# Prompt attention of a hybrid decoder layer: the reciprocals of the row sums, and the factors of the compressed branch, made by GpSimd as powers of minus one instead of by VectorE

## The reference, cut to what matters

```python
def masked_softmax(s, mask):
    s = jnp.where(mask, s.astype(jnp.float32), -1e30)
    m = jnp.max(s, -1, keepdims=True)
    p = jnp.where(mask, jnp.exp(s - m), 0.0)
    return p / jnp.maximum(jnp.sum(p, -1, keepdims=True), 1e-30)
...
    p_c = masked_softmax(jnp.einsum('bqkgd,bnkd->bqkgn', q, kc) * scale, m_c)      # 63 compressed blocks
    p_s = masked_softmax(jnp.einsum('bqkgd,bkqmd->bqkgm', q, ks) * scale, m_s)     # selected blocks
    p_w = masked_softmax(jnp.einsum('bqkgd,bwkd->bqkgw', q, kw) * scale, m_w)      # window of 512
    return gates[..., 0:1] * o_c + gates[..., 1:2] * o_s + gates[..., 2:3] * o_w
```

## Time and profile before

| | |
|---|---|
| runs of the kernel before | 1854.03, 1854.60, 1855.23 us |
| span of the profiled execution | 1851.3 us |
| the stage of the prompt attention in it | about 680 to 1160 us |
| TensorE busy in the whole span | 1811.8 us, 98% |
| VectorE | 1178.0 us, 64% |
| ScalarE | 938.0 us, 51% |
| GpSimd | 471.1 us, 25% |

### The profile page before, as it was taken

One profiled execution on the slowest core, in us unless ns is written; L12 is line 12 of the kernel. 1 busy time (PEld: TensorE's weight loads), 2 busy tenths in 40 slices (PEclk: granted clock), 3 DMA queues, 4 the chain that ended last, 5 costly groups with the idle time before them and its releaser, 6 DMA issues.

```text
span 1851.3 us, 32100 instructions
## 1 busy us (share of the span) xinstructions
PE 1811.8 (98%) x11821; PEld 1617.9 (87%) x11822; DVE 1178.0 (64%) x1673; ACT 938.0 (51%) x1574; POOL 471.1 (25%) x627
## 2 busy tenths in 40 slices
PE   8999999999999999999999999999999999999998
PEld 8999999789999878888988898998867888888884
DVE  5744444556221379999999999644477686744756
ACT  4333344113021278888898888411133676645756
POOL 0000000000000025555555554002212454322431
PEclk9999999999999999999999999999999999999999
DMA  5234334214241640000000000535246797877875
GB/s 183 86 104 116 102 98 162 80 46 128 86 147 38 218 112 1 1 2 1 2 2 2 1 1 8 168 89 172 93 195 247 286 392 296 289 272 234 317 241 195
DMA packets 119762, 241.08 MB, mean 130 GB/s; under 512 B 27986, under 2 KB 84858, under 8 KB 113466
## 3 DMA queue, kind: packets, MB, share of 16 engines
q1 hardware_dynamic: 112666, 214.26, 33.0%
q0 software_dynamic: 6976, 25.17, 5.5%
HBM read 193.52 MB, written 45.88 MB: 129 GB/s over the span
## 4 chain that ended last, share of the span: by engine, by line
PE 53%; DVE 5%; ACT 3%; issue 1%; POOL 1%; DMA 0%; POOLq 0%; ACTq 0%; DVEq 0%
PE ps L3450 20%; PE ps L2169 6%; PE ps L2195 5%; PE ps L3032 4%; PE ps L263 4%; PE ps L2141 3%; PE ps L2143 3%; PE ps L3438 1%; DVE small L2286 1%; PE ps L2133 1%; PE ps L3499 1%; ACT turned_high L2397 1%; PE ps L2212 1%; ACT region_w L2386 1%; DVE turned_low L2310 1%
## 5 line engine op out<-in xcount | busy, mean ns | idle before, releaser
L2286 DVE TENSOR_REDUCE small<-ps 128x1 f32<-128x640 f32 (+7 forms) x256 | 179.5, 703 | 25.4 <-PE ps L2133 23.6
L2310 DVE TENSOR_TENSOR turned_low<-ps,turned_high 128x512 fp32r<-128x512 f32 (+2 forms) x304 | 176.6, 614 | 11.5 <-ACT turned_high L2397 7.3
L2465 POOL TENSOR_SCALAR region_w<-region_w,small,gates 128x640 f32<-128x640 f32 (+7 forms) x172 | 141.0, 831 | 127.8 <-DVE small L2290 127.7
L2397 ACT CAST turned_high<-ps 128x512 fp32r<-128x512 f32 (+2 forms) x304 | 156.3, 530 | 30.5 <-PE ps L2169 26.4
L2195 PE MATMUL ps<-turned_high,value_stacks 128*128 128x256 f32 (+1 forms) x608 | 160.4, 294 | 0.1
L2141 PE MATMUL ps<-key_stacks,query_stacks 128*128 128x256 f32 (+3 forms) x384 | 140.6, 366 | 13.3 <-ACT region_w L2386 6.7
L2195 PE MATMUL ps<-turned_low,value_stacks 128*128 128x256 f32 (+1 forms) x608 | 149.2, 282 | 0.0
L2386 ACT ACTIVATE region_w<-ps,small 128x640 f32<-128x640 f32 (+7 forms) x172 | 121.6, 707 | 23.8 <-DVE small L2286 19.9
L3450 PE MATMUL ps<-down_parts,hidden_parts 128*128 128x512 f32 x552 | 131.1, 393 | 0.0
L3450 PE MATMUL ps<-up_parts,rows_parts 128*128 128x512 f32 x552 | 129.1, 389 | 0.1
L3450 PE MATMUL ps<-gate_parts,rows_parts 128*128 128x512 f32 x528 | 126.0, 394 | 0.0
(11 more groups left out here) (558 smaller groups left out, 4900.5 us busy)
## 6 DMA issues: line engine op xcount, KB each, us to landing
region_k<-in_w_gate SPq DMA_DIRECT2D x16, 2048.0 KB, 9.3
region_k<-in_w_up SPq DMA_DIRECT2D x16, 2048.0 KB, 10.9
region_w<-in_w_down SPq DMA_DIRECT2D x16, 2048.0 KB, 13.9
region_w<-in_w_in SPq DMA_DIRECT2D x14, 512.0 KB, 4.3
region_k<-in_w_in SPq DMA_DIRECT2D x10, 512.0 KB, 4.3
small<-gate_a SPq DMA_DIRECT2D x8, 516.0 KB, 3.5
region_w<-gate_b SPq DMA_DIRECT2D x8, 516.0 KB, 4.1
region_k<-in_x_prompt SPq DMA_DIRECT2D x8, 512.0 KB, 7.7
```

Source lines behind the costliest of these rows:

```text
L2286: nc.vector.tensor_reduce(nmax[:, n % 4:n % 4 + 1], sc, AX.X, ALU.max, negate=True).then_inc(s_max, 1)
L2310: nc.vector.tensor_tensor(lo, m.ps[:, turn_bank(G), 0:w], hi, ALU.subtract).then_inc(s_lo, 1)
L2397: nc.scalar.copy(hi, m.ps[:, turn_bank(G), 0:w]).then_inc(s_hi, 1)
L2465: nc.gpsimd.tensor_scalar(probs(H, t), probs(H, t), rec[:, H % 4, t:t + 1], m.gates[:, 2 * p + t, col:col + 1], ALU.mult, ALU.mult).then_i ...
```

## The change

VectorE no longer makes reciprocals. GpSimd raises the row sums to the power of minus one, element by element, with a `tensor_tensor` whose second input is a small constant tile of minus ones (`minus_one`, 128x8, filled once). For a half that is one instruction of 128x2 numbers at the head of `scale`, which waits for the exponentials themselves (`s_exp`) and no longer for VectorE's `s_rec`. For the compressed branch VectorE keeps only the sum (`compressed_total`). The maximum with 1e-30 (even `c`), the power (128x8) and the product with the gates are three GpSimd instructions at the head of `compressed_scale`. Each of the new instructions is waited for by the next one through a semaphore.

```diff
-        def reciprocals(H):
-            dve.wait_ge(s_exp, n_of[H, 1] + 1)
-            nc.vector.reciprocal(rec[:, H % 4, :], sums[:, H % 4, :]).then_inc(s_rec, 1)
...
-        def compressed_gain(c):
-            q, j = c % 2, c // 2
-            done = 5 * j + 3 * q
+        def compressed_total(c):
+            q = c % 2
             dve.wait_ge(s_cp, c + 1)
+            if c >= 2:
+                dve.wait_ge(s_cgain, gain_steps(c - 2))
             nc.vector.tensor_reduce(csum[q], pc_rows[:, 8 * q:8 * q + 8, 0:NCMP], AX.X, ALU.add).then_inc(s_csum, 1)
-            dve.wait_ge(s_csum, done + 1)
-            if q == 0:
-                nc.vector.tensor_scalar(csum[q], csum[q], 1e-30, None, ALU.max).then_inc(s_csum, 1)
-                dve.wait_ge(s_csum, done + 2)
-            nc.vector.reciprocal(crec[q], csum[q]).then_inc(s_csum, 1)
-            dve.wait_ge(s_csum, done + (3 if q == 0 else 2))
-            gate = m.gates[:, 4 * q:4 * q + 4, 3 * j:3 * j + 25:24]
-            nc.vector.tensor_tensor(cgain[q].rearrange("p (i g) -> p i g", g=NKV),
-                                    crec[q].rearrange("p (i g) -> p i g", g=NKV), gate, ALU.mult).then_inc(s_cgain, 1)
...
         def scale(H):
             j, p, g, a = half(H)
-            pool.wait_ge(s_rec, H + 1)
+            col = 24 * g + 3 * j + 1 + a
+            pool.wait_ge(s_exp, n_of[H, 1] + 1)
+            nc.gpsimd.tensor_tensor(gain[:, H % 4, :], sums[:, H % 4, :], minus_one[:, 0:2], ALU.pow).then_inc(s_gain, 1)
+            pool.wait_ge(s_gain, H + 1)
             for t in range(2):
-                col = 24 * g + 3 * j + 1 + a
-                nc.gpsimd.tensor_scalar(probs(H, t), probs(H, t), rec[:, H % 4, t:t + 1],
+                nc.gpsimd.tensor_scalar(probs(H, t), probs(H, t), gain[:, H % 4, t:t + 1],
                                         m.gates[:, 2 * p + t, col:col + 1], ALU.mult, ALU.mult).then_inc(s_scaled, 1)
 
         def compressed_scale(c):
-            q = c % 2
+            q, j = c % 2, c // 2
             x = pc_rows[:, 8 * q:8 * q + 8, :]
-            pool.wait_ge(s_cgain, c + 1)
+            pool.wait_ge(s_csum, c + 1)
+            if q == 0:
+                nc.gpsimd.tensor_scalar(csum[q], csum[q], 1e-30, None, ALU.max).then_inc(s_cgain, 1)
+                pool.wait_ge(s_cgain, gain_steps(c) - 2)
+            nc.gpsimd.tensor_tensor(cgain[q], csum[q], minus_one, ALU.pow).then_inc(s_cgain, 1)
+            pool.wait_ge(s_cgain, gain_steps(c) - 1)
+            cg = cgain[q].rearrange("p (i g) -> p i g", g=NKV)
+            nc.gpsimd.tensor_tensor(cg, cg, m.gates[:, 4 * q:4 * q + 4, 3 * j:3 * j + 25:24], ALU.mult).then_inc(s_cgain, 1)
+            pool.wait_ge(s_cgain, gain_steps(c))
             nc.gpsimd.tensor_tensor(x, x, cgain[q].unsqueeze(2).to_broadcast([P, 8, 64]), ALU.mult).then_inc(s_scaled, 1)
...
         nc.clear_and_free_semaphores(done)
+        nc.gpsimd.memset(minus_one, -1.0).then_inc(s_pc, 1)
         nc.gpsimd.memset(pc_rows[:, :, NCMP:64], 0.0).then_inc(s_pc, 1)
+        pool.wait_ge(s_pc, 1)
```

More of the change, by code:

```diff
@@ L2055, in attend_prompt @@
     sums = m.small[:, 4:12].rearrange("p (h t) -> p h t", t=2)
-    rec = m.small[:, 12:20].rearrange("p (h t) -> p h t", t=2)
+    gain = m.small[:, 12:20].rearrange("p (h t) -> p h t", t=2)
     cmax = m.small[:, 32:40]
-    csum, crec, cgain = ([m.small[:, 40 + 16 * x + 8 * q:48 + 16 * x + 8 * q] for q in range(2)] for x in range(3))
+    csum, cgain = ([m.small[:, 40 + 16 * x + 8 * q:48 + 16 * x + 8 * q] for q in range(2)] for x in range(2))
     identb, diag, edge = m.identb, m.mask_diag, m.mask_edge
@@ L2067, in attend_prompt @@
     s_qk, s_exp = lw.s_scores, lw.s_probs
-    s_max, s_rec, s_scaled = (m.sem("a_" + n) for n in ("max", "reciprocal", "scaled"))
-    s_cmax, s_csum, s_cgain = m.sem("a_c_max"), m.sem("a_c_sum"), m.sem("a_c_gain")
+    s_max, s_gain, s_scaled = (m.sem("a_" + n) for n in ("max", "gain", "scaled"))
+    s_cmax, s_csum, s_cgain = m.sem("a_c_max"), m.sem("a_c_sum"), m.sem("a_c_gain_steps")
+    minus_one = m.small[:, 72:80]
     s_cs, s_ch, s_cd, s_cp = (m.sem("a_c_" + n) for n in ("scores", "sums_of_parts", "differences", "probs"))
@@ L2073, in attend_prompt, with gain_steps @@
     lw.turns, lw.turned_last_but_two, lw.turned_last_but_one = len(turns), turned_by(NHALF - 3), turned_by(NHALF - 2)
+    def gain_steps(c):
+        return 5 * (c // 2) + 3 + 2 * (c % 2)
     def refill(H):
@@ L2257, in compressed_sum @@
                 else:
-                    dve.wait_ge(s_pc, 1)
+                    dve.wait_ge(s_pc, 2)
             at = 8 * q + 4 * s
@@ L2330, in _ @@
                 compressed_sum(compressed_of(H + 2), 0)
-            if 0 <= H + 1 < NHALF:
-                reciprocals(H + 1)
             if H == 1:
@@ L2355, in _ @@
             if H == 0:
-                compressed_gain(0)
+                compressed_total(0)
             for c in (early(H + 1), late(H + 1, 1)):
                 if c is not None and c != 0:
-                    compressed_gain(c)
+                    compressed_total(c)
         lw.b.low(dve, 0)
```

## The result

The changed kernel takes 1897.45 us (median of 4 runs, 1894.65 to 1903.16), the kernel before 1854.91 on the same chip: a ratio of 1.0237, 95% interval 1.0219 to 1.0254. It is slower, as forecast, but by 42.5 us and not by 12, outside the range that ended at 1886. The four runs of the changed kernel lie 8.5 us apart: the fastest had a mean granted clock of 0.995 of full speed, the slowest one of 0.989.

A forecast was written before the change was run, and what follows sets the result against it. TensorE bounds the attention stage's heavy part, a chain through all queues its light part. Lateness 1.56 - 0.08 = 1.48 us a period, times 8 = 11.8, plus 0.1 to 0.3 at entry: 1854.6 + 12.1, say 1867 us; range 1846 to 1886.

The forecast's parts named there:

- The light part is where the cost arises, and GpSimd's reciprocal waits were paid by hardly anybody.: Attention period's stretch of short halves: all growth falls here; TensorE waited only 8.2 us for GpSimd's scalings.
- heavy part: Attention period's stretch where TensorE sets the time, busy 38.93 of 39 us in the fourth; can't take time back.
- The light end is 1.81 us late at the turn of 49.: Half 49, behind the even compressed branch: turn starts at 871.29 against 869.48, with powers of 1.10 and 0.65 us.
- At 52 it shrinks to 1.56.: Half 52: scaling starts 0.78 us behind its exponentials, at 877.23 against 875.67, so its turn is 1.56 us late.
- The odd compressed branch ... brings the turn of 56 some 1.5 us late, under the 1.56 that TensorE is late already.: Odd branch, about 883.4 us, ahead of halves 55 and 56: its delay hides under TensorE's existing lateness, adding nothing.
- The halves' powers are hidden where GpSimd is free.: Usual halves: scalings that find GpSimd free come no later, covering most of the 128 powers, about 83 us.
- The port.: Rival, chance 0.13: GpSimd's scalings block VectorE's `output` at SBUF, 1.5 us a period, 12 us on top, 1879 us.
- Dear columns.: Rival, chance 0.14: compressed power's eight columns cost like eight powers; 1885 us by the middle price, up to 1902.

The follow-up runs named there:

- e8: Kernel before, but only halves H mod 16 = 0, 4, 5, 6, 12 get their power on GpSimd; 1857.78 us, ratio 1.0023.
- e10: Kernel before, nothing on GpSimd, each half's reciprocal one place earlier in VectorE's queue; 1860.36 us, ratio 1.0031.
- e11: Kernel before, reciprocal one place earlier in VectorE's queue only for halves H mod 16 = 4, 5, 6, 8, 12; 1854.43 us, ratio 1.0003.
- e3: Kernel before, but only the eight even compressed factors (maximum, power, product) made by GpSimd; 1870.45 us, ratio 1.0089.
- e1: Changed kernel, but VectorE makes the compressed factors again and only the 128 halves' powers stay on GpSimd; 1867.58 us, ratio 1.0071.
- e4: Kernel before, but only the eight odd compressed factors (power, product) made by GpSimd; 1858.91 us, ratio 1.0025.
- e2: Kernel before, but even and odd compressed factors made by GpSimd, halves keeping VectorE's reciprocals; 1874.26 us, ratio 1.0110.
- e7: Kernel of e1, but every fourth half (H mod 4 = 3) keeps VectorE's reciprocal; 1864.35 us, ratio 1.0062.
- e6: Changed kernel with five useless matmuls ahead of TensorE's wait for each even compressed turn; 1892.75 us, ratio to before 1.0214.
- e5: Changed kernel with the 16 powers of 128x8 replaced by products of the same shape; 1917.0 us with other experts chosen, stage 496.4 against 524.1 us.
- e9: Kernel before, plus probe powers and products of 1 to 32 columns on idle GpSimd at program start; powers 0.39 us plus 0.155 a column up to eight.

## Why the prediction was wrong

Point by point, in its order:

- *The light part is where the cost arises, and GpSimd's reciprocal waits were paid by hardly anybody.* The second is right: an early scaling gave nothing in e8, e10 and e11. The first is half right: of the 5.3 us a period 2.65 arise at the light end, the rest at mod 16 = 7 and 8 and at 11 and 12, in what I had called the heavy part, where I expected no growth.
- *The light end is 1.81 us late at the turn of 49.* The mechanism was right, the term under-sized: 2.65 us, because the power of 128x8 takes 1.66 us and not 1.10 (0.56), that of 128x2 0.70 and not 0.65, VectorE's sum ended 0.15 later in the period (1.79 us behind its start for 1.64; I had it 0.08 earlier), and handovers and maximum a little more. e3 and e1 split it into 1.70 and 0.94. Put into my sum, the two measured powers give 2.14 us a period and 1872 us in all. The sizes are 5 us of the miss, and the steps below are the rest.
- *At 52 it shrinks to 1.56.* Wrong: 2.63. I had `queries` end 0.2 us ahead of the exponentials, so that the scaling follows these 0.78 us later. In the period from `H` = 64 the exponentials ended at 963.80, `queries` at 963.98 and the scaling began at 964.75, 0.95 us behind the exponentials, as long as before.
- **The step that failed: "The odd compressed branch ... brings the turn of 56 some 1.5 us late, under the 1.56 that TensorE is late already."** This takes the larger of two delays, which holds only if the inputs of the odd branch keep their old times. They come from TensorE's scores and shift with it: in e3, where only the even branch moved, the odd branch's sum ended 17.60 us into the period and not 15.90, as late as TensorE. So what a later place adds goes on top. e3 and e4 show it (1.69 + 0.72, and 2.42 in e2), and the changed kernel loses 2.26 us there: 0.72 by the odd branch, 0.36 by the halves' powers, and 1.2 more where the two meet in one full stretch of GpSimd. That is 18 us that my sum had at nothing, more than my whole forecast.
- *The halves' powers are hidden where GpSimd is free.* True in the middle, not at `H` mod 16 = 1 and 8, where GpSimd comes from other work (0.94 and 0.36 us in e1), nor at 4 in e8 (0.43). e1: 13.7 us.
- *The port.* A rival of mine at 12 us; real, but some 4 us (e7), since the lateness grows by it at one of a period's four `output`s only. The Trainium skill, "SBUF — State Buffer", section "Who interferes with whom", calls the port that both want an exclusive lock, and says that the order of issue decides who blocks. The trace agrees: `output`, the later of the two, took 0.98 us in place of 0.40 and ended 0.26 us behind the scaling it had begun in.
- *Not in the prediction: the clock.* 8.3 us of the profiled stage (e6): three periods are 1.7 to 2.0 us longer than 65.4, and the first is 2.6 longer than in e6.
- *Dear columns.* Chance 0.14. The slope is 0.155 us a column, between my 0.08 and the 0.34 of that rival. That its upper end, 1902 us, lies near the measured time is luck: it took 4.56 us for the power of 128x8, which takes 1.65. e5 puts this power at 27.7 us with the clock, against a product of its size. By my sum, in which only the even branch pays, the measured difference of 1.45 us would be worth 8 x 1.45 = 11.6. So the length was the smaller error, and where it is paid for the larger.

The 47.3 us of the stage by these terms: the clock 8.3, by e6, where all else stays. Of the other 39.0 the six usual periods have 5.2 each, 31.2 in all, the first period has 3.1 and the last 4.6. The 5.3 us of a usual period in the changed kernel are 2.65 for the light end, 2.26 for the odd branch and the halves beside it and 0.55 for the port, less 0.13 that comes back.

## What to carry to other kernels

When a change makes one stage late, everything that depends on it moves along: a second delay further on hides behind the first only if its own inputs don't move. Write the new times of all inputs beside each other, or add the delays. Before moving a tiny operation to another engine, look for a row with the same number of columns: a fixed price read from one column can be a third of the real one. And a long wait of an engine that is off the path is no reason to shorten it.

## What the hardware showed that I had not expected

- A power on GpSimd costs 0.39 us and 0.155 us for each column of 128, up to eight; the product of 128x8 0.21 us, VectorE's reciprocal 0.20 (e9).
- One idle stretch of TensorE (busy 1.01 of 3 us) was followed by some 3.4 us at half clock, worth 1.9 us, in three of six usual periods with the same work; in the other three the same wait didn't lower it. The five useless matmuls removed it everywhere.
- A VectorE addition of 64x256 numbers from two SBUF tiles took 0.98 us in place of 0.40 when it began inside a GpSimd scaling, and the other way round a power of 128x16 took 1 us more than the line through the others when it began inside such an addition (e9, one row).
